# The last level of the RWKV inverse: 64 by 64 products for the off-diagonal block alone

## The reference, cut to what matters

```python
def step(S, inp):
    rt, wt, kt, vt, kkt, at = inp
    sa = jnp.einsum('bhvi,bhi->bhv', S, -kkt)
    S = S * wt[:, :, None, :] + sa[..., None] * (kkt * at)[:, :, None, :] + vt[..., None] * kt[:, :, None, :]
    return S, jnp.einsum('bhvj,bhj->bhv', S, rt)
```

## Time and profile before

| | |
|---|---|
| time before, median of 3 runs | 2096.95 us (2096.91 to 2098.89) |
| profiled execution: span | 2149.5 us (no other time is listed for it) |
| TensorE busy | 2058.8 us, 96% |
| VectorE, ScalarE, GpSimd busy | 45%, 38%, 47% |
| mean granted TensorE clock | 0.957 |
| RWKV chunks, layer 1 (350.16 to 536.29 us) | 186.13 us, mean granted clock 0.67 |
| RWKV chunks, layer 2 (1437.52 to 1571.93 us) | 134.41 us, granted clock 1.00 |

### The profile page before, as it was taken

How to read it: one execution, slowest core, us unless ns; L and a number is a source line. 1 busy time by engine, 2 the same in 40 slices (tenths; PEclk the granted TensorE clock), 3 DMA queues, 4 the chain that set the end, 5 groups by cost and what they waited for, 6 DMA issues and landing times.

```text
span 2149.5 us, 35579 instructions
## 1 busy us (share of the span) xinstructions
PE 2058.8 (96%) x12528; PEld 1645.8 (77%) x12528; DVE 967.0 (45%) x1801; ACT 818.8 (38%) x1395; POOL 1000.7 (47%) x1225
## 2 busy tenths in 40 slices
PE   7999999999999999999989999999999999999996
PEld 6876757777767888888887868567776888888885
DVE  6737865211334442232368379663333335223135
ACT  6434255112442622222355343463344354222235
POOL 4444524211536555555744445252144665555574
PEclk9999999656999999999999999999999999999998
DMA  5122301000212223333312223111121321332333
GB/s 180 60 79 71 97 30 50 30 21 21 72 57 88 79 79 108 98 98 98 108 50 78 70 79 99 50 40 41 31 66 53 108 79 60 108 97 92 96 97 118
DMA packets 53741, 163.17 MB, mean 76 GB/s; under 512 B 5312, under 2 KB 17728, under 8 KB 53312
## 3 DMA queue, kind: packets, MB, share of 16 engines
q1 hardware_dynamic: 52416, 158.09, 23.3%
q10 hardware_dynamic: 1152, 2.86, 0.4%
HBM read 158.83 MB, written 2.10 MB: 75 GB/s over the span
## 4 chain that ended last, share of the span: by engine, by line
issue 54%; POOL 43%; POOLq 1%; DVE 1%; ACT 1%; PE 1%; DMA 0%; SPq 0%; DVEq 0%; ACTq 0%
POOL w_lo L1619 37%; POOL slab L1643 3%; POOL slab L1664 1%; POOL wx_lo L1619 1%; POOL rstd L1632 1%; POOLq L1649 0%; POOL slab L1646 0%; DMA wx_raw<-wproj 0%; POOLq L1624 0%; DVE u_lo L1727 0%; DVE slab L1718 0%; ACT u_hi L1157 0%; PE bank L597 0%; PE bank L596 0%; PE bank L595 0%
## 5 line engine op out<-in xcount | busy, mean ns | idle before, releaser
L1619 POOL TENSOR_TENSOR w_lo<-w_raw,w_hi 128x256 fp32r<-128x256 f32 x1104 | 857.3, 808 | 1114.7 <-ACT w_hi L1166 834.8
L595 PE MATMUL bank<-hn_hi,w_hi 128*128 128x512 f32 (+1 forms) x1312 | 550.8, 420 | 1.5 <-ACT slab L1391 1.3
L596 PE MATMUL bank<-hn_lo,w_hi 128*128 128x512 f32 (+1 forms) x1312 | 516.9, 394 | 0.0
L597 PE MATMUL bank<-hn_hi,w_lo 128*128 128x512 f32 (+1 forms) x1312 | 516.7, 394 | 0.0
L595 PE MATMUL bank<-u_hi,w_hi 128*128 128x512 f32 (+1 forms) x864 | 308.3, 357 | 8.5 <-DVE u_lo L1741 5.5
L595 PEld LDWEIGHTS bank<-hn_hi,w_hi 128*128 128x128 f32 x1312 | 252.4, 192 | 75.4 <-issue 26.1
L597 PE MATMUL bank<-u_hi,w_lo 128*128 128x512 f32 (+1 forms) x864 | 303.4, 351 | 0.0
L596 PE MATMUL bank<-u_lo,w_hi 128*128 128x512 f32 (+1 forms) x864 | 303.1, 351 | 0.0
L597 PEld LDWEIGHTS bank<-hn_hi,w_lo 128*128 128x128 f32 x1312 | 253.6, 193 | 52.9
L596 PEld LDWEIGHTS bank<-hn_lo,w_hi 128*128 128x128 f32 x1312 | 254.2, 194 | 42.6 <-issue 3.8
L1550 ACT ACTIVATE w_hi<-w_raw 128x1024 fp32r<-128x1024 f32 x120 | 127.3, 1061 | 401.5 <-DMA w_raw<-wrest 401.3
(11 more groups left out here) (336 smaller groups left out, 2866.6 us busy)
## 6 DMA issues: line engine op xcount, KB each, us to landing
w_raw<-wrest SPq DMA_DIRECT2D x140, 512.0 KB, 3.5
w_raw<-wmerge SPq DMA_DIRECT2D x80, 512.0 KB, 3.5
w_raw<-wproj SPq DMA_DIRECT2D x60, 512.0 KB, 3.6
wx_raw<-wproj SPq DMA_DIRECT2D x6, 512.0 KB, 4.7
slab<-rope ACTq DMA_DIRECT2D x2, 1024.0 KB, 4.8
wx_raw<-wrest SPq DMA_DIRECT2D x4, 512.0 KB, 4.7
out<-x SPq DMA_DIRECT2D x4, 512.0 KB, 3.0
x<-x_in SPq DMA_DIRECT2D x2, 512.0 KB, 10.0
```

What stands on the lines that cost most here:

```text
L595: mm(o_, stat[0], mov[0], start=first, stop=False)
L596: mm(o_, stat[0], mov[1], start=False, stop=False)
L597: return mm(o_, stat[1], mov[0], start=False, stop=last)
L1619: ins = pool.tensor_tensor(wchunk(1, s_)[:, cs], wload(s_)[:, cs], wchunk(0, s_)[:, cs].bitcast(f32), SUB)
```

## The change

The loop over levels stops at 5, where all products are 64 by 64 as before. The last level is written out behind it. With `top` = partitions 0 to 63 and `low` = 64 to 127, the first product multiplies, for each head, the off-diagonal block of `LTm` with the upper left block of `X_`, into the lower half of bank 4. DVE copies this half as it stands, 64 partitions by 256 columns, without a mask, into `PPs[0]`. The second product multiplies that with the lower right block of `XT_`, into the upper half of bank 6, and ACT copies 64 by 64 by 4 heads into the upper right blocks of `XT_`. The identity that was restored in `PPs[0]` at level 5 is no longer written. Waits, semaphore counts of the products, and the dense steps between them stay as they were.

```diff
-                    for lv in range(1, 7):
+                    for lv in range(1, 6):
...
-                                if lv == 6:
-                                    hs, hh = slice(h * P, (h + 1) * P), slice(h * HD, (h + 1) * HD)
-                                    ins = mm(packed(bank_[:, hh], n), stat[:, hs], halves(mov[:, hs], n, side), start=True, stop=True)
-                                    continue
...
+                    top, low = slice(0, HD), slice(HD, P)
+                    pe.wait_ge(*c_xxu.at(L, 11 * c + 10))
+                    pe.sem_inc(carrier, 1)
+                    for h in range(H):
+                        h1, h2, hh = h * P, h * P + HD, slice(h * HD, (h + 1) * HD)
+                        ins = mm(ps[4][low, hh], LTm[top, h2:h2 + HD], X_[top, h1:h1 + HD], start=True, stop=True)
+                    ins.then_inc(*c_pp.up())
+                    dense(("c_level", c, 6, 0))
+                    pe.wait_ge(*c_ppu.at(L, 6 * c + 6))
+                    pe.sem_inc(carrier, 1)
+                    for h in range(H):
+                        h2, hh = h * P + HD, slice(h * HD, (h + 1) * HD)
+                        ins = mm(ps[6][top, hh], PPs[0][low, hh], XT_[low, h2:h2 + HD], start=True, stop=True)
+                    ins.then_inc(*c_xx.up())
+                    dense(("c_level", c, 6, 1))
...
-                            ins = fn(halves(tgt, n, side), packed(ps[bk][:, 0:256], n), ACT.Copy)
+                            ins = fn(heads(XT_)[0:HD, :, HD:P], ps[6][0:HD, 0:256].rearrange("p (h n) -> p h n", h=H), ACT.Copy)
...
+                        if lv == 6:
+                            dve.tensor_copy(PPs[0][HD:P, 0:256], ps[4][HD:P, 0:256]).then_inc(*c_ppu.up())
+                        else:
+                            carry_wait()
...
+                        if lv != 5:
+                            link(dve.tensor_copy(heads(PPs[(lv + 1) % 2]), over_heads(C("ident"))))
```

More of the change, by code:

```diff
@@ L389, in trunk_kernel @@
         hid_hi = signal("hidden_hi_ready", 8 * QUARTERS)
-        dve_step = signal("dve_step", 193)
+        dve_step = signal("dve_step", 189)
         act_step = signal("act_step", 9)
@@ L947, in _ @@
                         pe.sem_inc(carrier, 1)
-                        if lv < 6:
-                            level_product(ps[5], XT_, PP, 0).then_inc(*c_xx.up())
+                        level_product(ps[5], XT_, PP, 0).then_inc(*c_xx.up())
                         level_product(ps[6], PP, XT_, 1).then_inc(*c_xx.up())
                         dense(("c_level", c, lv, 1))
+                    top, low = slice(0, HD), slice(HD, P)
[13 more added lines that the diff above has]
+                    dense(("c_level", c, 6, 1))
                     pe.wait_ge(*c_st.at(L, c + 1))
@@ L2083, in _ @@
                         dve.wait_ge(*c_pp.at(L, 6 * c + lv))
[L2084 to L2090, removed]
+                        if lv == 6:
+                            dve.tensor_copy(PPs[0][HD:P, 0:256], ps[4][HD:P, 0:256]).then_inc(*c_ppu.up())
+                        else:
+                            carry_wait()
+                            n = LEVELS[lv]
+                            dve.copy_predicated(halves(PPs[lv % 2], n, 0).rearrange("p (h b) n -> p h b n", h=H),
+                                                level_half(1, lv, n, 0), packed(ps[4][:, 0:256], n)
+                                                .rearrange("p (h b) n -> p h b n", h=H)).then_inc(*c_ppu.up())
+                        if lv != 5:
+                            link(dve.tensor_copy(heads(PPs[(lv + 1) % 2]), over_heads(C("ident"))))
                         gated(("c_level", c, lv, 1))
```

## The result

| | before | changed |
|---|---|---|
| median of 20 executions each | 2098.27 us | 2112.95 us |
| lowest, highest | 2095.36, 2151.06 | 2094.40, 2130.47 |
| executions above 2104 us | 8 of 20 | 16 of 20 |
| profiled execution: time, span | not listed, 2149.5 | 2113.87, 2112.1 |

The ratio is 1.0052, 95% interval 1.0033 to 1.007: slower, by half a percent. It leaves out executions more than 1.5% above the fastest of their kernel, so most of the bad executions of the kernel before are not in it (six of eight, against two of sixteen of the changed kernel); therefore I count executions as well. The means of all 20 are the same for both kernels, 2111.7 us, and with the later executions they are 2108.5 (92 of the kernel before) and 2110.7 (30 of the changed one). So what the change made slower is the usual execution; averaged over all of them no difference is shown.

A forecast was written before the change was run, and what follows sets the result against it. TensorE was taken as the bound. At full clock, 1.44 + 1.47 - 2 x 1.17 = 0.57 us a chunk, 8 x 0.57 = 4.6, so 2096.95 - 4.6 = 2092.4 us; range 2090 to 2099.5.

The forecast's parts named there:

- The products: Two level 6 products a chunk: 0.61 us each instead of 0.89, 1.17 with surroundings instead of 1.44 and 1.47.
- Rival (a): New products: load and stream don't overlap on one quarter, product 0.83 us, gain 1.0, 2095.9 us; chance 0.11.
- rival (b): New products: one quarter as slow as the whole array, switch paid, product 1.04 us, 2099.1 us; chance 0.05.
- the 0.3 us for the wait: Second product's shorter wait for DVE, subtracted from the 2.4 us loss to give 2.1 in rival (b).
- The chunk: Each of eight RWKV chunks shortens by 0.57 us, all alike, from the second layer's times.
- the sum at full clock: Both RWKV stages: 8 x 0.57 = 4.6 us gained, all of it expected to reach the end.
- Copies and waits: Level 6: DVE's copy, some 0.45 us, stays hidden behind the dense step; 0.03 us of waiting goes; no wait is added.
- The clock: Both RWKV stages: timed executions assumed at full clock; the profiled first layer was 51.7 us longer, excess subtracted from the span.
- rival (d): RWKV chunks: moved starts and quarter-array work drop one more to half clock, 17.2 us, 2109.6 us; chance 0.10.
- P: Follow-up theory, not in the prediction: thin chunk starts let the clock fall; distance between chunks sets how often.
- Rival (c): Behind the stage: gain lost at a later wait, such as the start of attention, 2096 us; chance 0.07.

The follow-up runs named there:

- e5: Kernel before, whole-array products at level 6, three of eight head products a chunk left out; 7 of 12 executions fallen, 2104.9 to 2108.9 us with its repeat, others 2093.1 to 2097.3.
- e1: Changed kernel with head 0 computed again, five small quarter matmuls more a chunk; 9 of 12 executions at 2097.9 to 2104.5 us, others 2119, 2121 and 2138.
- e3: Kernel before with one dense step more before level 1 of each chunk; median 2096.49 us, ratio 0.9989, none of 12 executions fallen.
- e4: Changed kernel with the same dense step more before level 1 as e3; ratio 0.9974 to the kernel before, median 2091.5 us together with e10.
- e2: Kernel before with head 0 computed twice more in both level 6 products; 8 of 12 executions at 2103.7 to 2109.4 us, 4 at 2122 to 2129.
- e10: Same kernel as e4, run again for a narrower interval; ratio 0.997 to the kernel before, median 2091.5 us together with e4.

## Why the prediction was wrong

**The products: right.** I had 0.61 us for a product and 1.17 with its surroundings; measured 0.60, and 1.17 and 1.16. The argument (what counts is the larger of weight and moving columns, also on one quarter) held: e5 puts 128 moving columns on 128 weight columns and its chunk is 33.42 us, within 0.05 of 34.04 less six times 0.111; e1 gives the same 0.058 us for an instruction on a quarter. Rival (a) (0.83) and rival (b) (1.04) are out. (The 0.3 us for the wait in the price of (b) should be 8 x 0.03 = 0.24; nothing hangs on it.) The rule of the Trainium skill behind (b) (TensorE: Matmul & The Clock Gate, Part 3), that a load overlaps running products only when the row group differs, isn't borne out: eight loads into the same quarter came 0.058 apart. The Trainium skill's other rule (TensorEngine Tiling (Array Packing), Key Properties), that a change of tiling mode drains TensorE, fits the 0.60: eight instructions of 0.058 are 0.46, and 0.14 is left for entry and exit; no run sets a drain apart in it.

**The chunk: right but for one of four.** 0.57 us forecast, 0.60 measured for three chunks of a layer. The first chunk gained only 0.2 (34.33 to 34.12). There POOL adds branch results at the same time, DVE's operations on the state take longer beside it, and TensorE waits for them at line 916. The first two groups are the end of the first chunk in the changed kernel and in the kernel before, the third is the end of the second chunk of the changed kernel, where POOL does nothing:

```profile
1415.99 1.10 DVE L2115 TENSOR_SCALAR st<-st,col 128x64 f32<-128x64 f32 x2
1417.14 2.06 PE L916 MATMUL bank<-slab 64*128 64x128 f32 x32 [0.70 <-DVE st L2115]
```
```profile
1469.89 0.72 DVE L2102 TENSOR_SCALAR st<-st,col 128x64 f32<-128x64 f32 x2
1470.67 2.06 PE L916 MATMUL bank<-slab 64*128 64x128 f32 x32 [0.32 <-DVE st L2102]
```
```profile
1450.11 0.42 DVE L2115 TENSOR_SCALAR st<-st,col 128x64 f32<-128x64 f32 x2
```

So the sum at full clock was 2 x 2.0 = 4.0 us and not 4.6. POOL's additions overlap these two operations by 0.9, 0.5 and 0 us in the three, and they take 1.10, 0.72 and 0.42. No run was made for it, but in e3 and e4, where they no longer meet in the first chunk, the operations take 0.42 in both and the chunk gains the whole 0.6 (34.57 to 33.96).

**Copies and waits: right.** DVE's copy stayed hidden, the 0.03 us of waiting went.

**The clock: the step that failed.** "I take it that the timed executions held the full clock in both layers, and work the sum for full clock." For those three it was so. But the trace in front of me was an execution that hadn't held it, so of four executions known one had fallen; of 92 timed in all it was 29%. The likeliest execution was taken for the kernel, and the clock entered the sum with nothing. The change took the share of fallen executions from 29% to 77% (23 of 30), at 17.4 us for a fallen chunk, over four times what the products save. What the change does to that share was then left to rival (d) with 0.10, on the ground that no timed run showed it and TensorE stays as busy as it was. Rival (d) was the right mechanism and nearly the right time (2109.6 against 2112.95): it named the start of the chunks moving by half a microsecond. It also named the quarter of the array, which a fall doesn't need: the kernel before and e5 fall without it. By the times, the kernel before mostly falls several chunks at a time (23 of its 27 lie at 2132 us and above) and the changed one mostly a single chunk (20 of 23 at 2110 to 2115). P reads this as chunks that keep their place, fallen 51.3 and upright 34.04 us apart, against chunks that wander. That reading isn't shown: e1 has the distance of before and fell singly twice, and e2 has another and fell no more often.

**The rest.** Rival (c) is out: e4 against e3 has the whole gain in the time. Of the four plus three upright executions of the changed kernel (2094.4 to 2100.5), the median is 2096.5, only 1 us under the upright ones of before where 4 were due; the same few us lie on e1. A lower clock goes with it: of these seven the two fastest had a mean granted clock of 0.987 over the whole execution, the next four 0.985, and the slowest 0.983, while of the 53 upright ones of before that have it listed all but one had 0.987 to 0.989. So there are low stretches elsewhere in the program; which, and why, wasn't tried.

**Open:** what, besides the thin start, decides whether a chunk falls; why 33.44 us falls in 23 of 30 executions and 34.93 only in 4 of 12; and whether the quarter products add to it (23 of 30 against 10 of 18).

## What to carry to other kernels

When a profile's granted clock is low in some stretches and full in others with the same instructions, the kernel's time is a mixture; count executions on each step before pricing an edit, and expect that a change in the distance of repeated stages can change the odds. Look at the mean of all executions beside the median. Look for the stretch just ahead of the fall: where TensorE waits in a stage of small products, move a dense product there first. That made the saving of a few tenths of a microsecond per chunk visible at all, and it was worth more than the saving: by the means of all executions, 12 us (2108.5 to 2096.3 in e3) against 5.

## What the runs showed of the hardware that I had not expected

- A chunk behind a stretch with TensorE busy 2.5 of 3.4 us fell to half clock in some executions and stayed there for 41 us while TensorE's records show it busy throughout; no gap in that stretch was longer than 0.73 us. With one dense step more (3.24 of 3.40 busy in three chunks of a layer, 2.69 in the first) it never fell in 25 executions of e3, e4 and e10.
- The cost of the thinner start: one dense step of 0.7 us taken from each of eight chunks made the kernel 134 us slower (2097.9 to 2232.2).
- fp32 products on a single quarter of the array, 64 weight columns by 64 moving columns: 0.058 us for each listed instruction, the same as two halves in turn reach in each half, and half of the 0.111 of 128 weight columns by 64 moving.
- DVE's unmasked copy of 64 partitions took 0.43 us against 0.45 for the masked one of 128, 256 columns each: mask and partitions together made 0.02.
